# The second gate applied to each expert's rows on GpSimd, and the final sums moved off TensorE

## What is computed

```python
h2 = modulate(rmsnorm(x, g_norm2), sh2, sc2)
# top-1 of 4 groups, top-2 of 8 gated-MLP experts in it; gate: one number per token and choice
y[e] = (silu(xs @ w_gate[e]) * (xs @ w_up[e])) @ w_down[e]     # rows of one expert
moe[token] = gate[0] * y_first + gate[1] * y_second
x = x + gt2 * moe                                              # gt2: a vector over the 1024 channels
out = rmsnorm(x, g_final)
```

## Time and profile before

| | |
|---|---|
| median of three runs | 1292.8 us |
| the profiled execution | 1292.83 us, its span 1291.0 us, mean granted TensorE clock 0.981 |
| TensorE, VectorE, ScalarE, GpSimd busy | 95%, 72%, 55%, 19% of the span |
| the experts | from about 657 to 1239 us |
| the finish block | from 1245.1 us to the end |

### The profile page before, as it was taken

How to read it: one execution, slowest core, us unless ns; L and a number is a source line. 1 busy time by engine, 2 the same in 40 slices (tenths; PEclk the granted TensorE clock), 3 DMA queues, 4 the chain that set the end, 5 groups by cost and what they waited for, 6 DMA issues and landing times. The chain is left out here.

```text
span 1291.0 us, 18692 instructions
## 1 busy us (share of the span) xinstructions
PE 1232.0 (95%) x7306; PEld 1024.4 (79%) x7306; DVE 934.3 (72%) x1105; ACT 706.7 (55%) x827; POOL 249.9 (19%) x201
## 2 busy tenths in 40 slices
PE   4799999999999999999989999999999999999966
PEld 1799888888788888888878888888888888888852
DVE  2656544332688887556669998989989888989847
ACT  3832212112556665322247777878787877778723
POOL 0000000001101000000011542623535265321001
PEclk8899999999999999999899999999999999999988
DMA  9648844434577772600559999999999999999756
GB/s 379 239 181 295 283 149 157 159 114 164 201 234 160 170 181 81 235 36 34 180 198 354 383 392 390 374 392 376 384 384 377 393 377 390 380 383 386 252 195 262
DMA packets 94459, 343.81 MB, mean 266 GB/s; under 512 B 17387, under 2 KB 45731, under 8 KB 66723
## 3 DMA queue, kind: packets, MB, share of 16 engines
q1 hardware_dynamic: 74499, 311.37, 65.8%
q10 hardware_dynamic: 10656, 14.43, 3.8%
q0 software_dynamic: 9216, 16.80, 3.5%
HBM read 313.70 MB, written 39.33 MB: 273 GB/s over the span
## 5 line engine op out<-in xcount | busy, mean ns | idle before, releaser
L2010 DVE TENSOR_TENSOR w_low<-raw,w_high 128x2048 fp32r<-128x2048 f32 x128 | 293.4, 2313 | 30.8 <-ACT w_high L1950 28.0
L1950 ACT ACTIVATE w_high<-raw 128x2048 fp32r<-128x2048 f32 x128 | 241.1, 1910 | 9.6 <-DVEq L1312 9.6
L2010 DVE TENSOR_TENSOR w_low<-arena,w_high 128x2048 fp32r<-128x2048 f32 x64 | 146.4, 2290 | 31.6 <-ACT w_high L1950 31.6
L1950 ACT ACTIVATE w_high<-arena 128x2048 fp32r<-128x2048 f32 x64 | 122.1, 1908 | 3.2 <-DMA arena<-in_w_down 3.2
L1909 POOL DMA_INDIRECT y_rows<-arena,row x32 | 48.1, 1504 | 324.2 <-ACT arena L1971 322.6
L1867 PE MATMUL p_g<-w_high,x_high 128*128 128x512 f32 x252 | 101.7, 404 | 2.0 <-DVE w_low L2010 1.1
L1867 PE MATMUL p_u<-w_high,x_high 128*128 128x512 f32 x256 | 102.3, 400 | 0.0
L1867 PE MATMUL p_a<-tokens_high,half_high 128*128 128x512 f32 (+1 forms) x272 | 101.8, 374 | 0.2 <-DVE half_low L698 0.2
L1868 PE MATMUL p_a<-tokens_low,half_high 128*128 128x512 f32 (+1 forms) x272 | 100.9, 371 | 0.0
L1869 PE MATMUL p_a<-tokens_high,half_low 128*128 128x512 f32 (+1 forms) x272 | 100.8, 371 | 0.0
L1869 PE MATMUL p_u<-w_high,x_low 128*128 128x512 f32 x256 | 100.0, 391 | 0.0
(11 more groups left out here) (344 smaller groups left out, 2823.4 us busy)
## 6 DMA issues: line engine op xcount, KB each, us to landing
raw<-in_w_gate SPq DMA_DIRECT2D x64, 1024.0 KB, 8.3
raw<-in_w_up SPq DMA_DIRECT2D x64, 1024.0 KB, 7.9
arena<-in_w_down SPq DMA_DIRECT2D x64, 1024.0 KB, 8.4
raw<-in_w_ada SPq DMA_DIRECT2D x24, 1024.0 KB, 7.8
x<-qk_rows SPq DMA_DIRECT2D x6, 1664.0 KB, 9.0
raw<-in_w_chunks SPq DMA_DIRECT2D x9, 1024.0 KB, 5.8
qk_rows<-x SPq DMA_DIRECT2D x18, 512.0 KB, 2.6
yy<-y_rows SPq DMA_DIRECT2D x8, 1024.0 KB, 13.5
```

The lines of the kernel that those rows point to most:

```text
L1950: act.activation(x.high[i % SPLITS][:], x.raw[j][:, :], ACT.Copy).then_inc(high_ok, 1)
L2010: dve.tensor_tensor(x.low[i % SPLITS][:], x.raw[j][:, :], x.high[i % SPLITS][:], ALU.subtract).then_inc(low_ok, 1)
```

## The change

1. gate2 as a row vector goes to HBM with the three other vectors (from ScalarE, in the attention), and is loaded onto all partitions once, behind the loads of expert 1. For experts 0 to 30 GpSimd multiplies the output buffer by it, in place, and then scatters. ScalarE still moves y for these. For expert 31 VectorE multiplies while it reads PSUM, and ScalarE's move is left out.
2. Experts, spare blocks and finish become one block. SP waits for one semaphore, `all_rows`, before it loads the expert rows. The final gain is loaded behind the tables of expert 27. The finish uses the experts' buffers.
3. In the finish, TensorE has nothing to do. For tiles 0 to 6 VectorE begins (first row times its routing gate, plus x1), ScalarE multiplies the second row by its routing gate, and GpSimd adds. For tile 7 VectorE does both. The last pair of tiles has a root and a refinement for each tile.

```diff
-NORMS = [(0, 2), (2, 2), (4, 2), (6, 2)]
+NORMS = [(0, 2), (2, 2), (4, 2), (6, 1), (7, 1)]
...
-        STORE_AT = {2 * NT + 2: 0, 3 * NT + 2: 1, 4 * NT + 2: 2}
+        STORE_AT = {2 * NT + 2: 0, 3 * NT + 2: 1, 4 * NT + 2: 2, 4 * NT + 6: 3}
...
-                sp.wait_ge(s.first_in, 112)
+                sp.wait_ge(s.first_in, 128)
...
+                if (n, j) == (1, 3):
+                    sp.dma_start(x.gate2[:], a.vec_rows[3:4, :].to_broadcast([P, D])).then_inc(c_in, 16)
+            sp.wait_ge(over_listed, 1)
+            sp.dma_start(x.over_work[:], a.g_final.to_broadcast([P, D])).then_inc(c_in, 16)
+            sp.wait_ge(low_ok, len(order))
+            spare.sync(sp)
+            last.sync(sp)
...
                 pool.wait_ge(y_ok, n + 1)
+                if n < NE - 1:
+                    pool.tensor_tensor(x.y[b], x.y[b], x.gate2[:], ALU.mult).then_inc(y_scaled, 1)
+                    pool.wait_ge(y_scaled, n + 1)
                 pool.indirect_dma_start(a.y_rows, bass.IndirectOffsetOnAxis(ap=s.row[:, n:n + 1], axis=0), x.y[b], None,
...
             scatter(NE - 1)
+            count = spare.count(pool)
             for b in range(2):
                 pool.wait_ge(scattered[b], 16 * (NE // 2))
+            spare.gpsimd(pool, count)
+            pool.sem_inc(q.all_rows, 1)
+            last.gpsimd(pool)
...
-            move_y(NE - 1)
+            act.wait_ge(over_ready, over.STEPS)
+            spare.scalar(act, spare.count(act))
+            last.scalar(act)
...
+            dve.wait_ge(used, place[NE - 1, 5] + 1)
+            halves = lambda y: y.rearrange("p (c n) -> p c n", c=2)
+            dve.tensor_tensor(halves(x.y[(NE - 1) % 2]), x.p_y[:], halves(x.gate2[:]), ALU.mult).then_inc(y_ok, 1)
+            spare.vector(dve, spare.count(dve))
+            last.vector(dve)
...
+    def gpsimd(pool):
+        c = Counter(pool, refined)
+
+        def add(i):
+            pool.wait_ge(gated, i + 1)
+            pool.wait_ge(begun, i + 1)
+            pool.tensor_tensor(s.x1[:, i, :], s.x1[:, i, :], yy[i][:, 1, :], ALU.add).then_inc(added, 1)
...
+        for i in range(POOLED):
+            add(i)
+            if i in (2, 4, 6):
+                refine(i // 2 - 1)
+
+    def scalar(act):
+        def gate(i):
+            act.wait_ge(y_in[i], 16)
+            act.activation(yy[i][:, 1, :], yy[i][:, 1, :], ACT.Copy, scale=s.gates[:, 1, i:i + 1]).then_inc(gated, 1)
...
+        gate(0)
+        for i in range(NT):
+            if i + 1 < POOLED:
+                gate(i + 1)
+            square(i)
...
+        def begin(i):
+            dve.wait_ge(y_in[i], 16)
+            dve.scalar_tensor_tensor(s.x1[:, i, :], yy[i][:, 0, :], s.gates[:, 0, i:i + 1], s.x1[:, i, :], ALU.mult, ALU.add).then_inc(begun, 1)
+
+        def end(i):
+            dve.wait_ge(begun, i + 1)
+            dve.scalar_tensor_tensor(s.x1[:, i, :], yy[i][:, 1, :], s.gates[:, 1, i:i + 1], s.x1[:, i, :], ALU.mult, ALU.add).then_inc(ended, 1)
...
+        for i in range(4):
+            begin(i)
+        invert(0)
+        begin(4)
+        scale(0)
+        begin(5)
+        invert(1)
+        begin(6)
+        scale(1)
+        begin(7)
+        end(7)
+        invert(2)
+        scale(2)
+        for g in (3, 4):
+            invert(g)
+            refine(g)
+            scale(g)
```

More of the change, by code:

```diff
@@ L2139, in _ @@
                     for u in range(2 * NT):
[L2140 to L2142 removed]
+                        placed = pe.matmul(x.p_list[:, 0:2 * OVB], over.match[:, u, :], over.code[:, u].rearrange("p d b -> p (d b)"),
+                                           start=(u == 0), stop=(u == 2 * NT - 1))
+                    placed.then_inc(over_listed, 1)
                 if n == 0:
@@ L2159, in _, with spare_blocks, count_of, each @@
                 for k in range(KE):
-                    last = pe.transpose(x.p_h[:, k, :], every(x.h, k, KE), s.ident[:])
-                last.then_inc(h_turned, 1)
+                    turned = pe.transpose(x.p_h[:, k, :], every(x.h, k, KE), s.ident[:])
+                turned.then_inc(h_turned, 1)
             last_downs()
-def spare_blocks(nc, t, a, s, x, q):
+            spare.tensor(pe, spare.count(pe))
+def spare_blocks(t, a, s, x, q):
+    spare = Buffers()
     picked, freed, passed = t.sem("picked"), t.sem("freed"), t.sem("passed5")
-    def each(engine, body):
-        count = engine.value_load(s.blocks[0:1, OVB:OVB + 1], min_val=0, max_val=OVB)
+    def count_of(engine):
+        return engine.value_load(s.blocks[0:1, OVB:OVB + 1], min_val=0, max_val=OVB)
+    def each(engine, count, body):
         with engine.If(count > 0):
@@ L2175, in each @@
                 body(n)
[L2177 to L2246, removed]
-                        k = 4 * (j % 2) + i
-                        last = pe.matmul((x.p_g, x.p_u)[j // 2][:], x.x_whole[:, k, :], x.raw[j][:, i * DE:(i + 1) * DE],
-                                         start=(k == 0), stop=(k == KD - 1))
-                    if j % 2 == 1:
-                        last.then_inc(q.used, 1)
-                pe.wait_ge(q.h_ok, n + NE + 1)
-                for k in range(KE):
-                    last = pe.transpose(x.p_h[:, k, :], every(x.h, k, KE), s.ident[:])
-                last.then_inc(q.h_turned, 1)
-                pe.wait_ge(q.h_high, n + NE + 1)
-                for j in (4, 5):
-                    pe.wait_ge(q.loaded[j], (n + NE + 1) * 16)
-                    for h in range(2):
-                        for i in range(2):
-                            k = 2 * (j - 4) + i
-                            last = pe.matmul(x.p_y[:, h, :], x.h_whole[:, k, :], x.raw[j][:, i * D + h * 512:i * D + (h + 1) * 512],
-                                             start=(k == 0), stop=(k == KE - 1))
-                last.then_inc(q.used, 1)
-            each(pe, body)
@@ L2469, in build @@
         experts(nc, a, s)
-        finish(nc, a, s)
 def query_order(x):
```

281 lines of the change are left out of this document (151 added, 130 removed).

## The result

The changed kernel took 1334.52 us (median of 4 runs, 1327.07 to 1335.8) against 1293.06 us for the kernel before beside it: a ratio of 1.0296, 95% interval [1.0274, 1.0319]. I had forecast 1304.5 with a range up to 1320; the direction was right, the size was not, and the time lies outside the range. The profiled execution took 1333.81 us with a span of 1331.9, 40.9 us more than the span before.

The account below looks back on a forecast made before the run. The prediction took TensorE to bound the experts, with VectorE the engine with least room, and VectorE to bound the finish. 1292.8 + 9 (expert stage) + 2.7 (finish) = 1304.5 us, range 1286 to 1320.

Parts of the forecast that it names:

- part 1: Expert loop: GpSimd's 31 multiplies hold VectorE up, gather delay of 2.4 us stays hidden; stage +9 us.
- rival 1: Expert loop: multiply waits for VectorE's PSUM reads, or costs under 1.85 us of idle time; total 1296 us, chance 0.16.
- +4: Expert loop: multiply makes VectorE's expert 18.0 us against TensorE's 17.76, less a 2.8 us lead; +4 us.
- +5: Spare blocks' tables on GpSimd, in eight experts: no longer hidden by VectorE's 1.85 us of room; +5 us.
- Part 2: Block boundaries before the finish: first load goes out 1.7 us earlier (0.7 to 2.0).
- Part 3: Final sums in the finish: VectorE's operations and GpSimd's adds exclude each other; +2.7 us, the 1.7 us earlier load included.
- Rival 2: Finish: the last sums don't exclude each other, -8.5 us, stage as forecast; total 1293.3 us, chance 0.12.

Follow-up runs that it names:

- ahead: Changed kernel with the gather of a later expert issued ahead of multiply, scatter and table steps; 1298.61 us, ratio 1.0046 to the kernel before.
- tail_dve: Against ahead: the finish's GpSimd adds and ScalarE gates left away, VectorE does begin and end of every tile; 1293.55 us, ratio 1.0000 to the kernel before.
- after2: The changed kernel run once more with no edit; 1329.54 us, ratio 1.0259 to the kernel before.
- after: The changed kernel itself, as first measured; 1334.52 us, ratio 1.0296 to the kernel before.
- nomul: Changed kernel without GpSimd's 31 multiplies and the wait behind each; 1297.64 us, ratio 1.0028 to the kernel before.
- double: Against ahead: each of the 31 GpSimd multiplies runs twice; 1362.31 us, ratio 1.0527 to the kernel before.

## Why the prediction was wrong, point by point

**The step that failed** is the sentence in part 1 that the gather's 2.4 us of delay are hidden. I had looked at a plain expert, where the gather stands right behind the scatter. In eight experts the tables stand between them; in five of these the rows then arrived only 1.4 to 4.3 us ahead of their step, and the delay was 7.3 to 9.8 us, not 2.4. The row that would have told it, the gather at 1100.77 behind 17.32 us of table steps, was in the trace of before. I had taken GpSimd's low busy share as room on its queue; but the gather stood behind everything that the program put in front of it. `ahead` shows it: order alone takes away 33 us.

**The price on VectorE** in part 1 had the right mechanism and was mis-sized: 2.2 us, not 2.47, so 15.5 + 2.2 = 17.7 fits into 17.76 where I had 18.0. So a plain expert pays 0 for the multiply, as the second clause of rival 1 had it (a multiply under the room), and the terms of +4 and +5 together are 1.6 to 3.7 us in `ahead` and tail_dve; rival 1's 1296 is near the 1298.6 of `ahead`. The first clause was wrong: the multiply didn't wait for a PSUM operation, the split behind it was held up as forecast (3.98 us where I wrote 4.6).

**The tables' +5** were put in the wrong place. Their share of those 1.6 to 3.7 us wasn't separated; VectorE takes 4.5 us from them, and that goes onto the queue ahead of the gather.

**Part 2.** Forecast 1.7 us earlier from scatter to first load, measured 5.54 - 3.48 = 2.06.

**Part 3.** Forecast +2.7 us for the last scale against the end of the experts: before 1287.88 - 1239.60 = 48.28, after 1327.59 + 1.28 - 1277.86 = 51.01, so +2.7, and the tail as a whole +2.6. (My own terms gave 1290.5 - 1287.88 = 2.6.) The path of 42.0 us from the first data to the last scale took 1328.87 - 1286.34 = 42.5. That it came out so close is luck in part: the exclusion took 13.2 us from VectorE where I had 16.6, and VectorE waited 5.8 us for loads, roots and inverse roots where I had 1.5. The begin beside an add took 2.41 us where I wrote 3.6, since the add had begun a us earlier; two scales around two adds took 6.76. Rival 2, no exclusion in the last sums, falls with `tail_dve`. The Trainium skill, "SBUF — State Buffer", section "Who interferes with whom", says that a VectorE instruction with two SBUF inputs contends with a GpSimd instruction that reads SBUF; the trace agrees, for the scalar_tensor_tensor too (2.41 us beside an add, 1.29 without).

**The lower clock** had no term. In the changed kernel's profile a wait of TensorE of 4.26 to 8.28 us cost another 1.7 to 2.4 us behind it, and the ones of 2.28 and 2.56 us 0.1. That doesn't give a rule by length: in after2 a wait of 2.52 us cost another 1.7 (granted clock 0.91) and one of 3.65 us 2.5 (0.87).

What stays open: the 3.0 us in the last expert. Some 2 of them go with a lower granted clock: the stretch took 40.98 us at 0.96 in after and 40.95 at 0.96 in tail_dve, but 39.05 at 1.00 in after2 and 38.91 at 1.00 in `ahead`. Beside the other 1 us stands a load of down weights that lands late (ScalarE waits 5.84 us for it, 3.23 before). `ahead` has 5.30 and `nomul` 3.49, so it goes with the multiplies; that VectorE's later splits free the weights' buffers later is not shown.

## What to carry to other kernels

Before work is put on an engine that also issues DMAs, list what its queue holds in front of each DMA in every variant of the loop, not in the common one, and compare the landing with the step that needs it; a busy share of 22% said nothing here, a landing 1.8 us ahead of its use said all. Issue the gather first. And count what GpSimd reads from SBUF at full length against VectorE: 2.4 us on GpSimd were worth offloading only if VectorE would have needed more than 2.2 us for it, and out of PSUM it needed 1.1.

## What the runs showed of the hardware

- A waiting GpSimd tensor_tensor got its turn between two of VectorE's splits that followed each other at once, and took a little less of VectorE's time (2.2 us) than it lasts (2.4), in `double`. The tensor_scalar at 1033.23 didn't: it took 4.70 us beside an undisturbed pair.
- The indirect DMA after a GpSimd multiply begins 0.80 us behind the multiply's end (0.78 to 0.82), and takes 2.25 us of GpSimd in the median; before, without the multiply, its median was 1.49.
- The gather's rows took 9.8 to 10.8 us to arrive in the five places that matter here, four times the 2.5 us of the issue, with 381 and 393 GB/s moved meanwhile in the last two; over all 32 gathers of the kernel before it was 4.3 to 13.1, in the median 10.8.
- Two float matmuls of 128x512 against a diagonal, for each of two halves, take 3.43 us of TensorE at the full clock, nearly three times VectorE's 1.25 us for one of the two scaled additions.
